# A hybrid encoder layer: the gates' and the router's products in four column groups

## What is computed

```
h = RMSNorm(x)*(1+scale1)+shift1
proj = h @ w_in
q_m, k_m, v_m, o_m, gates, q_n, k_n, v_n = split(proj)
hm = mLSTM heads forward and backward (q_m, k_m, v_m, gates), gated by sigmoid(o_m)
hn = neighbourhood_attention(q_n, k_n, v_n)
x = x + gate1 * RMSNorm([hm | hn] @ w_out)
h = RMSNorm(x)*(1+scale2)+shift2
aff = softmax(h @ w_router)            # 16 experts
gate, idx = top_k(aff.T, 128)          # each expert takes 128 tokens of a group
y = SwiGLU of each expert on its tokens, weighted, added back
x = x + gate2 * RMSNorm(y)
```

## Time and profile before

| | us |
|---|---|
| median of 3 runs | 2653.25 (2651.57 to 2654.32) |
| profiled execution | 2654.15, span 2652.4 |
| TensorE busy | 2342.2 (88%) |
| VectorE, ScalarE, GpSimd busy | 1202.8 (45%), 1085.1 (41%), 602.7 (23%) |
| mean granted TensorE clock | 0.943 of 2.4 GHz |
| gates' products (line 1662) | 96 x 0.23 apart |
| router's products (line 1746) | 16 tiles x 8 products |
| last router product starts / last `affT` copy / first load of the experts | 1348.8 / 1353.9 / 1358.3 |

### The profile page before, as it was taken

One profiled execution on the slowest core, in us unless ns is written; L12 is line 12 of the kernel. 1 busy time (PEld: TensorE's weight loads), 2 busy tenths in 40 slices (PEclk: granted clock), 3 DMA queues, 4 the chain that ended last, 5 costly groups with the idle time before them and its releaser, 6 DMA issues. The chain is left out here.

```text
span 2652.4 us, 34909 instructions
## 1 busy us (share of the span) xinstructions
PE 2342.2 (88%) x13256; PEld 1951.3 (74%) x13256; DVE 1202.8 (45%) x1832; ACT 1085.1 (41%) x1721; POOL 602.7 (23%) x606
## 2 busy tenths in 40 slices
PE   4799999898999997998922999999999999999950
PEld 2469988776899886777812788888888888888840
DVE  2121244554323435664566455544554455454516
ACT  3222344554433435663420444444444444444412
POOL 1102341342133343442331011111111111111013
PEclk8899999999999998999956999999999999999985
DMA  5464545656454576655452566666666666666629
GB/s 224 154 210 146 166 147 171 170 139 165 123 188 136 172 192 200 197 154 173 152 216 105 177 210 221 214 213 216 211 219 202 213 206 220 211 210 221 191 45 382
DMA packets 234969, 496.07 MB, mean 187 GB/s; under 512 B 36601, under 2 KB 127609, under 8 KB 231777
## 3 DMA queue, kind: packets, MB, share of 16 engines
q1 hardware_dynamic: 196704, 414.34, 46.7%
q0 software_dynamic: 35840, 71.74, 10.0%
q10 hardware_dynamic: 2304, 8.39, 0.8%
HBM read 405.41 MB, written 88.51 MB: 186 GB/s over the span
## 5 line engine op out<-in xcount | busy, mean ns | idle before, releaser
L2164 DVE TENSOR_TENSOR moe_w_lo<-moe_wf,moe_w_hi 128x2048 fp32r<-128x2048 f32 x192 | 439.9, 2292 | 550.4 <-ACT moe_w_hi L2086 550.4
L2086 ACT ACTIVATE moe_w_hi<-moe_wf 128x2048 fp32r<-128x2048 f32 x192 | 368.0, 1916 | 620.3 <-PE moe_acc L2217 601.5
L2217 PE MATMUL moe_acc<-moe_w_hi,moe_x_hi 128*128 128x512 f32 x1024 | 402.4, 393 | 6.9 <-ACT moe_hid L2100 5.5
L2217 PE MATMUL moe_acc<-moe_w_hi,moe_x_lo 128*128 128x512 f32 x1024 | 399.7, 390 | 0.0
L2217 PE MATMUL moe_acc<-moe_w_lo,moe_x_hi 128*128 128x512 f32 x1024 | 399.4, 390 | 0.0
L2217 PEld LDWEIGHTS moe_acc<-moe_w_hi,moe_x_hi 128*128 128x128 f32 x1024 | 192.9, 188 | 46.8 <-issue 6.0
L1673 PE MATMUL banks<-fr_w_hi,fr_h_hi 128*128 128x256 f32 x768 | 225.6, 294 | 0.0
L2217 PEld LDWEIGHTS moe_acc<-moe_w_hi,moe_x_lo 128*128 128x128 f32 x1024 | 192.8, 188 | 40.5
L2217 PEld LDWEIGHTS moe_acc<-moe_w_lo,moe_x_hi 128*128 128x128 f32 x1024 | 192.9, 188 | 39.2
L1664 PE MATMUL banks<-fr_h_hi,fr_w_hi 128*128 128x512 f32 x512 | 215.6, 421 | 3.7 <-DVE fr_w_lo L1270 2.1
L1673 PE MATMUL banks<-fr_w_lo,fr_h_hi 128*128 128x256 f32 x768 | 218.6, 285 | 0.0
(11 more groups left out here) (238 smaller groups left out, 4228.0 us busy)
## 6 DMA issues: line engine op xcount, KB each, us to landing
moe_wf<-in_w_expert_gate SPq DMA_DIRECT2D x64, 1024.0 KB, 4.9
moe_wf<-in_w_expert_up SPq DMA_DIRECT2D x64, 1024.0 KB, 4.8
moe_wf<-in_w_expert_down SPq DMA_DIRECT2D x64, 1024.0 KB, 5.0
fr_w_raw<-in_w_units SPq DMA_DIRECT2D x28, 1024.0 KB, 6.9
fr_bias<-in_na_bias SPq DMA_DIRECT2D x16, 1520.0 KB, 11.2
fr_a_w<-in_w_ada POOLq DMA_DIRECT2D x16, 1024.0 KB, 11.8
scratch_qk_t<-fr_stage SPq DMA_DIRECT2D x64, 256.0 KB, 2.5
scratch_vov<-fr_stage SPq DMA_DIRECT2D x96, 128.0 KB, 2.1
```

The source lines that it names most:

```text
L2086: nc.scalar.activation(w_hi[:, q, :, :], wf[:, q, :, :], ACT.Copy).then_inc(w_hi_ready, 1)
L2164: nc.vector.tensor_tensor(w_lo[:, q, :, :], wf[:, q, :, :], w_hi[:, q, :, :].bitcast(F32), ALU.subtract).then_inc(w_lo_ready, 1)
L2217: mm = nc.tensor.matmul(acc[:, j, b, :], x[:, g, k, :], w[:, q, a, h * HALF:(h + 1) * HALF], start=(k == 0 and i == 0), stop=(k == KC - 1 ...
```

## The change

The gates become one block in place of two: 8 k-steps x high and low part of h x four column groups. The weights stay unsplit fp32 (`wg`), the parts of h are read as plain fp32, column group j takes tokens 256j to 256j+255 and writes partitions 32j to 32j+15. The block stands behind the first block of token half 1. Its result is stored with four transfers. The router swaps its operands: 32 router columns (16 and 16 zeros) are the weights, 128 tokens move; column group j takes k = j and k = j+4. ScalarE copies the four groups' sums to SBUF (`lT`), and one product with `lT` as weights and `pick` (four stacked identities of 16) adds them as tokens by experts. The turn of the affinities and its copy move to ticks 5 and 7 of a tile, VectorE's work around them moves too, and `OUT_TAIL` is 3.

The diff, cut to its core:

```diff
@@ proj_plan and the times
-                    order = [(base + h, f, 0) for h in range(2) for f in range(2)] + [(GATE_UNIT, 0, t) for t in range(2)]
-                    order += [(base + h, f, 1) for h in range(2) for f in range(2)]
+                    order = [(base + h, f, t) for t in range(2) for h in range(2) for f in range(2)]
+                    order.insert(5, (GATE_UNIT, 0, 0))
...
-TURN_AT = {2: M1 - 2, 3: M1 + 3}
+TURN_AT = {2: (M1 - 2) * TICKS, 3: (M1 + 2) * TICKS + 3}
-LEAD_AT = [(M0 + 24) * TICKS, (M1 + 24) * TICKS]
+LEAD_AT = [(M0 + 23) * TICKS, (M1 + 23) * TICKS]
...
-        OUT_TAIL = 4
+        OUT_TAIL = 3
@@ SyncE
-                    sp.dma_start(io["gates_t"][g, :, t * HALF:(t + 1) * HALF], stage[0:GATES, b % 2, :]).then_inc(stored[b % 2], 16)
+                    for j in range(4):
+                        sp.dma_start(io["gates_t"][g, :, j * QW:(j + 1) * QW], stage[32 * j:32 * j + GATES, b % 2, 0:QW]).then_inc(stored[b % 2], 16)
@@ GpSimd: a new function, called once in the second mLSTM
+            def router_consts():
...
+                nc.gpsimd.memset(w_router[:, :, N_EXPERTS:], 0.0).then_inc(row_zeroed, 1)
+                nc.gpsimd.tensor_tensor(pick[:, :], ident[:, 0:N_EXPERTS], ident[:, 32:32 + N_EXPERTS], ALU.add)
@@ ScalarE
-                    if t >= 4:
-                        act.wait_ge(a_turned, t - 3)
-                        need(act, aff_stored, 16 * (t - 4))
-                        nc.scalar.activation(affT[:, :], ps[0:N_EXPERTS, PX, 0:P], ACT.Copy).then_inc(aT_ready, 1)
...
                     if t < N_TILES:
                         take_y(t, 0)
+                    if 2 <= t <= N_TILES + 1:
+                        act.wait_ge(l_parts, t - 1)
+                        nc.scalar.activation(lT[:, :], ps[:, PX, 0:P], ACT.Copy).then_inc(lT_ready, 1)
...
+                    if t >= 3:
+                        act.wait_ge(a_turned, t - 2)
+                        act.wait_ge(l_ready, min(t - 1, N_TILES))
+                        need(act, aff_stored, 16 * (t - 3))
+                        nc.scalar.activation(affT[:, :], ps[0:N_EXPERTS, PX, 2 * P:3 * P], ACT.Copy).then_inc(aT_ready, 1)
...
-            nc.scalar.activation(wg_hi[:, :, :], wg_raw[:, :, :], ACT.Copy).then_inc(wg_hi_ready, 1)
@@ VectorE: sum and scale of tile t-3 from tick 0 to tick 3, maximum and subtraction from tick 5 to tick 6
-            nc.vector.tensor_tensor(wg_lo[:, :, :], wg_raw[:, :, :], wg_hi[:, :, :].bitcast(F32), ALU.subtract).then_inc(wg_lo_ready, 1)
@@ TensorE
-                        if kind == "g":
-                            mm = nc.tensor.matmul(ps[0:GATES, b % 2, :], wg[x1][:, k, :], h[x2][:, k, t * HALF:(t + 1) * HALF], start=start, stop=stop)
+                    if kind == "g":
+                        for i, part in enumerate(h):
+                            for j in range(4):
+                                mm = nc.tensor.matmul(ps[32 * j:32 * j + GATES, b % 2, 0:QW], wg[:, k, :], part[:, k, j * QW:(j + 1) * QW].bitcast(F32),
+                                                      start=(k == 0 and i == 0), stop=(k == KC - 1 and i == 1))
...
-                        if u == 7 and 3 <= t <= N_TILES + 2:
...
+                        if u == 5 and t >= 3:
+                            turn_aff(t - 3)
+                        if u == 5 and 2 <= t <= N_TILES + 1:
+                            add_parts(t - 2)
...
-                    mm = nc.tensor.matmul(ps[:, PX, 0:N_EXPERTS], h2T[:, k, :], w_router[:, k, :], start=(k == 0), stop=(k == KC - 1))
-                mm.then_inc(l_done, 1)
+                    j = k % 4
+                    mm = nc.tensor.matmul(ps[32 * j:32 * j + 32, PX, 0:P], w_router[:, k, :], h2T[:, k, :], start=(k < 4), stop=(k >= 4))
+                mm.then_inc(l_parts, 1)
...
+            def add_parts(t):
...
+                pe.wait_ge(lT_ready, t + 1)
+                nc.tensor.matmul(ps[:, PX, P:P + N_EXPERTS], lT[:, :], pick[:, :], start=True, stop=True).then_inc(l_done, 1)
```

118 lines of the change are left out of this document (65 added, 53 removed).

## The result

The changed kernel takes 2659.84 us (median of 22 runs, 2653.56 to 2666.13), the kernel before 2653.87 us in runs beside it (22 runs, 2646.51 to 2659.49). The ratio is 1.0023, with a 95% interval of 1.0015 to 1.0030: **slower by 6 us**. The forecast was 2643.5 us with a range of 2633 to 2653. It was wrong, in sign as well.

What follows compares the result with a forecast made beforehand. TensorE was taken to bound the projections and output tiles 8 to 15. The terms -8.0 + 0.7 + 3.2 - 5.6 + 1.2 + 0.4 - 1.6 = -9.7 us from the median 2653.25 gave 2643.5 us, range 2633 to 2653.

Steps and rivals of the forecast that it cites:

- Gates, -8.0: Projections, both groups: one gates block takes 7.0 us for 11.0 where TensorE is never idle, saving 8.0 us.
- narrow weight loads set the pace: Rival, chance 0.07: 16-column loads do not overlap across column groups, gates cost 12.0 us for 11.0; result slower, 2667 us.
- What the missing block moves, +3.9: Projections: shorter block list adds waits, +0.7 us for the second half of h and +3.2 at the second mLSTM.
- Router, output tiles 8 to 15, -5.6: Tiles without attention: shorter router products less the wait for ScalarE's copy and the sum, -0.7 us a tile, eight tiles.
- I followed one tile: Step for tiles 8 to 15: one tile traced on ScalarE and TensorE, giving a 0.27 us wait for the copy.
- Router, tiles 2 to 6, +1.2: Output tiles under the attention: the attention's product comes 0.5 us later, less 0.25 from `affT`; five tiles, bounds -4 and +4.
- Tile 7 to 8, +0.4: Stall for the second group's mix: the router starts the chain of logits, h2, store and load, ending 0.4 us later.
- Tail, -1.6: Last router, at half clock: -3.59 + 1.05 for the router, +0.92 for signals, copy and sum, so 1.6 us saved.
- Behind the last `affT` copy: Top-k and experts: run as before; the forecast is wrong if this time moves by over 2 us.
- The copy takes the router's gain: Rival, chance 0.22: the sum waits longer for ScalarE, tiles 8 to 15 gain nothing; -2.8 us, 2650.5 us, no difference.
- TensorE's own time is all that counts: Rival, chance 0.13: the copy always lands before the sum and the two waits are hidden; -22 us, 2631 us.

Runs made afterwards that it cites:

- the best variant: Changed kernel with ScalarE's `lT` copy first under the attention, VectorE's affinity operations at tick 2 and the mix load ahead of the h2 store: 2641.11 us, ratio 0.9950.

## Why the prediction was wrong, step by step

**Gates, -8.0: right.** The block took 6.90 us for 7.0. (The forecast counts the step to four column groups as 0.1 us for both ways here, and as 0.1 each way at the router. TensorE's starts show 0.1 each way: the last full-width product at 107.35 and the first of four groups at 107.67 are 0.32 apart, for the usual 0.23.) The rival that narrow weight loads set the pace fell with that row.

**What the missing block moves, +3.9: the size about right, not by the right terms.** Router 1 stands at 1075.5 us on the mean of the nine profiles with the new gates, and at 1081.4 in the three with the old: -5.9, for -8.0 + 0.7 + 3.2 = -4.1. The second mLSTM's wait grew by 0.4 us in the two profiles, with 0.7 new ones for `qT`, and not by 3.2. (It scatters in the old kernels: 3.04, 1.43 and 1.77 us in the three profiles with the old gates, 3.3 to 3.5 in the nine with the new.) TensorE came there 5.6 us sooner relative to the attention's last store, the wait for `qT` left out (5.8 forecast), but E did so by 4.4 and not by 2.6: SyncE's loads are out 2.5 us sooner, and the work from them to E took 1.9 less. For the second half of h there was no wait at all. What I had not in the sum is the adaLN transfer: 3.4 or 3.5 us in the three profiles with the old gates, 7.7 to 8.1 with the new gates in each of the nine. Its cause is the shorter block list itself, which put a split of weights ahead of `a_row` in VectorE's queue: `a_row` starts at 156.8 to 157.1 us in the three and at 159.5 to 161.8 in the nine. In the first group, then, the whole gain of the gates was handed to that wait, and shorter waits for the attention's probabilities (27.6 us up to router 1 before, 23.3 now) gave about as much back.

**Router, output tiles 8 to 15, -5.6: wrong, +0.9 over seven of the eight periods** (0.1 to 0.9 in the five profiles that have this router and this loop). The terms for TensorE's own work were right: with the loop cut, the tiles come 13.07 us apart, as the sum said (13.1). The step that failed is "I followed one tile". I followed it on TensorE and ScalarE and asked only whether the copy is late for the sum. VectorE's logits wait for the sum, h2 stands behind the logits, the next mix behind h2, and the next router behind that mix. I had used this very chain in the paragraph on tile 7 to 8 and not asked if it also closes in the other tiles. The row of before that would have warned me is in the earlier trace rows: ScalarE waits 3.16 us for the mix and copies h2T only after splitting it, and the router starts at 1255.12, 0.05 us after the end of that copy:

```profile
1254.49 0.58 ACT L1052 ACTIVATE fr_h2T<-banks 128x512 f32<-128x512 f32 x1
```

From the router's start to the logits' row maximum are 1.89 us before in most tiles, and 2.70 now. TensorE was at 80 of 80 us with a neighbour on its heels. The loop is 13.97 us now and, by that difference of 0.8, was about 13.2 before (an estimate), under TensorE's 13.83. So a loop that got 0.8 us longer, while TensorE's work got 0.7 shorter, took the lead.

**Router, tiles 2 to 6, +1.2: the mechanism right, the size wrong, +11.1.** The term was 0.5 us for each slot: the queue of squares, probabilities, y and copy. The stop measured 1.4 to 2.1 us in four of the five (7.6 in all), and in the slot shown the attention's product came 1.2 us later after its slot's scores, not 0.5. The other 0.7 go with VectorE's three operations, whose move the sum had passed over: they stand right ahead of the row maximum, and the exponential starts 0.74 us later after the scores. That it would come back without them is not shown, as their move to tick 2 gave 0.15. The larger miss is the clock. It was at full speed there before, and I priced a stop as its length; three of them, and one of the stops for the probabilities, were followed by 3.4 to 6.8 us at half speed. The bound of +4 for this term was also too low, as it held no clock, and the bound of -4 should have been -4.9 by its own numbers (five times 0.97).

**Tile 7 to 8, +0.4: +1.5**, the wait 9.99 us for 7.93 before, by the chain of the earlier trace rows with the longer way to the logits in it. In the run that makes h2 ahead of the logits this wait is 7.99 us.

**Tail, -1.6: about right**, -0.8 and -1.3, so -2.1.

**Behind the last `affT` copy** I expected less than 2 us and the profile shows +3.9. Twelve profiles give 1298.3 to 1303.0 for that part, and the kernel before with the mix moved, which leaves it alone, has 1301.3. The work is the same; what differs in the rows is when the clock rises and falls. Behind the last `affT` copy it is low for 189.2 us before and for 199.8 in the changed kernel, and the twelve profiles lie between 188.9 and 200.5 us, in exactly the order of the time that this part takes. Part of it is the rise after the experts' start, as in the windows of 1440 to 1460 us before and after:

```profile
1440.00:1460.00 20.00, 18.39 (x81) 15.49 (x82) 6.57 (x6) 6.23 (x6) 2.10 (x3) 0.91 0.33 109
```

```profile
1440.00:1460.00 20.00, 15.21 (x60) 12.69 (x61) 4.87 (x5) 4.30 (x5) 2.09 (x3) 0.70 0.36 130
```

So I take these 4 us as scatter of the clock, which also may be why the profile's difference (7.4) and the measured one (6) are not the same. That the change has no part in it is likely, not shown.

**The rivals.** "The copy takes the router's gain" named the right engine at 2650.5 us. Of the 9.3 us that it lacks to 2659.8, 8.6 are in the attention's tiles (+11.1 for +2.5), where it left out the clock and VectorE's path. "TensorE's own time is all that counts" (2631) is what the best variant comes near to, at 2641, after three waits were moved away. The 0.07 for a slower result went to narrow weight loads, against which the gates' row speaks. A slower result by stops that cost the clock had no chance of its own in the forecast, and should have had one, since the change put a new wait of another engine on TensorE in the middle of the fullest stretch.

## What to carry to other kernels

When an engine is busy for all of a stretch, that says that it is the limit, not by how much: before counting its savings, follow the whole loop of one iteration, across the queues and the next transfer, and compare its length with the one of the busy engine. A new product that depends on another engine's copy needs that copy's place in the queue as much as the product itself; here the same change was 6 us slower with the copy behind squares, probabilities and y, and 13 us faster with the copy in front and the load taken out of the loop. A stop on TensorE of some 2 us at full speed can cost about twice its length (1.8 to 2.1 us and then half of 3.4), because the clock may fall behind it. And a list that all engines count by is shared: taking one block out of it changed the order of two operations in another engine's queue, and a wait far from the edit grew by 4.3 us.

## What the runs showed of the hardware

- **The clock after short stops.** In the changed kernel, stops of 1.8 us, 1.8 us (this one for the probabilities), 2.1 us and 1.8 us on TensorE, between stretches of full work, were each followed by 6.8, 3.4, 3.4 and 3.4 us at 1.2 GHz; one of 2.1 us (at 1068) and one of 1.4 were not. Of 14 stops for `lT` of 1.79 to 2.17 us in four kernels, 11 were followed by a fall, and of 24 for the probabilities of 1.74 to 2.14 us in twelve profiles, 11. The stops of under 0.8 us for `lT` were followed by none. The same stop for the probabilities at the same place (before 1072 us) in the same kernel was followed by 13.7 us in one execution and by 3.4 in another.
- **Four column groups in fp32.** 64 products of 256 columns passed in 6.90 us; 8 products of 128 columns with 32 columns of weights took 0.64 us in the row, for 1.85 for the form with 128 columns of weights and 16 moving ones. The loads of narrow weights did not hold them up: 128 of them one after the other at the 0.094 us of the earlier trace rows would have taken 12.0 us, not 6.90.
- **A transfer that comes later.** The adaLN weights landed for TensorE at 169.7 us in place of 166.2. GpSimd issued them 2.5 us later (163.24 for 160.75), and the first of them landed 6.45 us after its issue, for 5.38. The first is the order in VectorE's queue; why the landing itself took 1.1 us longer stays open.
